# A two-layer transformer kernel on one core: reordered opening loads and norm, and a stage join without a meeting of all engines

## The reference

```python
h = rms_norm(x, attn_norm)
proj = einsum('bsd,dc->bsc', h, w_in)          # split into 17 parts
... fox attention, short convolution, mLSTM, windowed attention with a relative bias ...
x = x + merged @ w_merge_out
h = rms_norm(x, ffn_norm)
x = x + (silu(h @ w_gate) * (h @ w_up)) @ w_down       # ffn1
```

## Time and profile before

| | |
|---|---|
| median of 3 runs | 1770.75 us (1769.94 to 1770.77) |
| profiled execution | 1771.35 us, its span 1769.6 us |
| PE busy | 97% of the span |
| DVE, ACT, POOL busy | 54%, 48%, 54% |
| first matmul | 12.84 us |
| mean granted TensorE clock | 0.992 |

### The profile page before, as it was taken

One profiled execution on the slowest core, in us unless ns is written; L12 is line 12 of the kernel. 1 busy time (PEld: TensorE's weight loads), 2 busy tenths in 40 slices (PEclk: granted clock), 3 DMA queues, 4 the chain that ended last, 5 costly groups with the idle time before them and its releaser, 6 DMA issues. The chain is left out here.

```text
span 1769.6 us, 27618 instructions
## 1 busy us (share of the span) xinstructions
PE 1714.8 (97%) x10430; PEld 1523.5 (86%) x10430; DVE 956.7 (54%) x1628; ACT 845.3 (48%) x1686; POOL 963.8 (54%) x701
## 2 busy tenths in 40 slices
PE   6999999999999999999979999999999999999998
PEld 4898887888888998999868978888988889989996
DVE  2147554454538761575048469994324398528842
ACT  4234454332336551464236348884534566426642
POOL 2353432334444874677336449993752368648852
PEclk9999999999999999999989999999999999999999
DMA  6332221123351433233324321012442223323431
GB/s 223 96 84 54 64 74 51 51 61 101 107 176 55 120 111 104 84 96 126 113 65 136 108 64 57 2 37 71 141 125 69 72 84 96 126 78 96 120 120 48
DMA packets 222900, 162.09 MB, mean 92 GB/s; under 512 B 9768, under 2 KB 197296, under 8 KB 222768
## 3 DMA queue, kind: packets, MB, share of 16 engines
q1 hardware_dynamic: 221712, 159.26, 30.2%
q10 hardware_dynamic: 1056, 1.06, 0.2%
HBM read 156.09 MB, written 2.11 MB: 89 GB/s over the span
## 5 line engine op out<-in xcount | busy, mean ns | idle before, releaser
L352 POOL TENSOR_TENSOR w_low<-ring,w_high 128x1024 fp32r<-128x1024 f32 (+2 forms) x223 | 487.9, 2192 | 587.5 <-ACT w_high L344 587.1
L365 PE MATMUL psum<-hT,w_high 128*128 128x512 f32 (+1 forms) x1104 | 378.9, 343 | 7.3 <-PEq L184 6.1
L344 ACT ACTIVATE w_high<-ring 128x1024 fp32r<-128x1024 f32 (+2 forms) x223 | 212.1, 954 | 355.1 <-PE psum L367 354.9
L367 PE MATMUL psum<-hT,w_low 128*128 128x512 f32 (+1 forms) x1104 | 373.2, 338 | 0.0
L366 PE MATMUL psum<-hL,w_high 128*128 128x512 f32 (+1 forms) x1104 | 373.0, 338 | 0.0
L365 PEld LDWEIGHTS psum<-hT,w_high 128*128 128x128 f32 x1104 | 209.9, 190 | 28.7 <-issue 7.3
L367 PEld LDWEIGHTS psum<-hT,w_low 128*128 128x128 f32 x1104 | 209.5, 190 | 22.8
L366 PEld LDWEIGHTS psum<-hL,w_high 128*128 128x128 f32 x1104 | 210.0, 190 | 19.8
L1819 POOL TENSOR_TENSOR w_low<-ffn_sums,w_high 128x512 fp32r<-128x512 f32 x120 | 169.4, 1426 | 49.7 <-ACT w_high L1814 49.5
L365 PE MATMUL psum<-ffn_th,w_high 128*128 128x256 f32 x640 | 181.6, 284 | 4.7 <-DVE ffn_g L2067 3.1
L1819 POOL TENSOR_TENSOR w_low<-ring,w_high 128x512 fp32r<-128x512 f32 x120 | 155.7, 1300 | 54.7 <-ACT w_high L1814 48.8
(11 more groups left out here) (443 smaller groups left out, 3758.7 us busy)
## 6 DMA issues: line engine op xcount, KB each, us to landing
ring<-in_w_in SPq DMA_DIRECT2D x58, 512.0 KB, 3.6
ring<-in_ffn_w_up SPq DMA_DIRECT2D x44, 512.0 KB, 3.8
ring<-in_w_gate SPq DMA_DIRECT2D x22, 512.0 KB, 3.7
ring<-in_w_up SPq DMA_DIRECT2D x22, 512.0 KB, 4.8
ring<-in_w_down SPq DMA_DIRECT2D x20, 512.0 KB, 3.7
ring<-in_ffn_w_down SPq DMA_DIRECT2D x20, 512.0 KB, 3.8
ring<-in_nsa_w_in SPq DMA_DIRECT2D x18, 512.0 KB, 3.6
ring<-in_ca_wkv SPq DMA_DIRECT2D x16, 512.0 KB, 3.6
```

Source lines behind the costliest of these rows:

```text
L344: nc.scalar.activation(tile_view(w_high, n, SPLIT), tile_view(ring, n, RING), ACT.Copy).then_inc(w_hi, 1)
L352: nc.gpsimd.tensor_tensor(tile_view(w_low, n, SPLIT), tile_view(ring, n, RING), tile_view(w_high, n, SPLIT), ALU.subtract).then_inc(w_lo, 1)
L365: nc.tensor.matmul(ps, lhsT=sh, rhs=mh, start=first, stop=False)
L367: return nc.tensor.matmul(ps, lhsT=sl, rhs=mh, start=False, stop=last)
```

## The change

In the opening:

- SP loads x tile 0, the gain, the identity alone and weight tile 0 first, then x tiles 1 to 3, weight tiles 1 and 2, then the rest of the constants.
- ACT takes a square root of a constant at once, which loads its function table.
- Weight tile 0 is split in two halves. PE turns token tile 0, does the products of weight tile 0 for it (`first_tile`), turns token tile 1, and so on.
- The matmul of the bias rows moves from the start to the head of chunk 2; ACT's write and read of them and DVE's mirrored copy move behind it, the copy to chunk 3.

At the join:

- The block is not closed and no meeting is held. The semaphores of the mixers are cleared by POOL inside ffn1, those of ffn1 in the cross attention.
- ffn1d1 leaves token tile 3 to the sparse stage, and `early` lets ACT split one weight tile more before the last token tile's square.
- The sparse stage starts with the left halves (token tiles 0 and 1) of its first feature tile, turns token tile 3, does the left half of the second, and then both right halves.

```diff
+        def stage_ends():
+            done = list(stage_sems)
             stage_sems.clear()
+            return done
...
+            early = early or whole is not None
...
-                            if whole is not None and t == tiles - 2:
+                            if early and t == tiles - 2:
                                 split_high(a, n0 + per - min(SPLIT, per) + SPLIT + 2)
...
         @block.tensor
-            pe.wait_ge(loaded, 48)
-            pe.wait_ge(misc, 16)
-            pe.wait_ge(zeroed, 2)
-            nc.tensor.matmul(bank[7][0:SWA_H, 0:384], lhsT=relT[:, :], rhs=const[0:BUCKETS + 1, C_OH:C_OH + 384],
-                             start=True, stop=True).then_inc(bias_mm, 1)
+            def first_tile(t):
+
+                pe.wait_ge(anorm.low, 2 * t + 1)
+                for kk in range(2):
+                    if kk == 0:
+                        pe.wait_ge(first_low, 1)
+                    else:
+                        pe.wait_ge(w_lo, 1)
+                    mm = chunk_product(0, 0, kk, t, first_split)
+                return mm
+
+            pe.wait_ge(ident_in, 16)
             for t in range(NT):
                 anorm.turn(pe, t)
+                if t < NT - 1:
+                    first_tile(t)
+            first_tile(NT - 1).then_inc(w_used, 1)
...
+                if c == 2:
+                    pe.wait_ge(loaded, 48)
+                    pe.wait_ge(misc, 16)
+                    pe.wait_ge(zeroed, 2)
+                    nc.tensor.matmul(bank[7][0:SWA_H, 0:384], lhsT=relT[:, :], rhs=const[0:BUCKETS + 1, C_OH:C_OH + 384],
+                                     start=True, stop=True).then_inc(bias_mm, 1)
...
         @block.scalar
+            nc.scalar.activation(stat[:, 151:152], eps, ACT.Sqrt).then_inc(warmed, 1)
+
+            def split_first():
+
+                wait_loaded(a, 0)
+                to, src = tile_view(w_high, 0, SPLIT), tile_view(ring, 0, RING)
+                nc.scalar.activation(to[:, 0], src[:, 0], ACT.Copy).then_inc(first_high, 1)
+                nc.scalar.activation(to[:, 1], src[:, 1], ACT.Copy).then_inc(w_hi, 1)
+                state["high"] = 1
+
+            for t in range(NT):
+                a.wait_ge(x_in[t], 16)
+                anorm.square(a, t, 0, D)
+                anorm.root(a, t)
+                if t == 0:
+                    anorm.high_part(a, 0, (0,))
+                    split_first()
+                    anorm.high_part(a, 0, (1,))
+                if t >= 2:
+                    anorm.high_part(a, t - 1)
+            split_high(a, 2)
+            anorm.high_part(a, NT - 1)
             split_high(a, SPLIT)
...
             for c in range(n_chunks):
+                if c == 2:
+                    bias_rows_out()
                 split_high(a, chunk_tile[c + 1] + SPLIT - 1)
+                if c == 2:
+                    bias_rows_back()
...
         @block.vector
+            for t in range(NT):
+                anorm.scale(v, t)
+                if t != 1:
+                    anorm.low_part(v, max(t - 1, 0))
+            anorm.low_part(v, NT - 1)
...
                 if c == 3:
+                    v.wait_ge(bias_in, 32)
+                    nc.vector.tensor_copy(bias[:, :, :], bias_back[:, :, ::-1])
                     v.wait_ge(rooted, 1)
...
         @block.sync
+            load_tokens(0)
             anorm.load(sp)
+            sp.dma_start(ident, w['const'][:, C_ID:C_ID + P]).then_inc(ident_in, 16)
+            load_weights(sp, 1 - RING)
+            for t in range(1, NT):
+                load_tokens(t)
+            load_weights(sp, 3 - RING)
+            sp.dma_start(const[:, P:C_END], w['const'][:, P:C_END]).then_inc(loaded, 16)
...
+                    if sems_done:
+
+                        nc.clear_and_free_semaphores(sems_done)
                     for operand in ("A11", "S2", "S1", "A12"):
                         seven.low(g_, r1, operand)
...
-        middle.close()
-
-        clear_stage()
...
-            for i in range(4):
+            pe.wait_ge(norm_n.low, NT)
+            products(n0, 0, slice(0, HALF))
+            norm_n.turn(pe, NT - 1)
+            products(n0 + 1, 1, slice(0, HALF))
+            pe.wait_ge(norm_n.low, 2 * NT)
+            for i in range(2):
+                products(n0 + i, i, slice(HALF, S)).then_inc(w_used, 1)
+            for i in (2, 3):
                 feature(n0 + i, i)
```

More of the change, by code:

```diff
@@ L457, in _parts, with high_part @@
                         self.dst[0][:, four, cut], self.dst[1][:, four, cut])
-            def high_part(self, a, t):
-                for c in range(2):
+            def high_part(self, a, t, parts=range(2)):
+                for c in parts:
                     src, high, _ = self._parts(t, c)
@@ L1036, in _ @@
                     wait_chunk_out(pe, c - 2)
[L1037 to L1039 removed]
+                if c == 2:
[4 more added lines that the diff above has]
+                                     start=True, stop=True).then_inc(bias_mm, 1)
+                for s in range(1 if c == 0 else 0, width // P):
+                    tile = tile_for(pe, chunk_tile[c] + s, 'w_in')
                     for kk in range(1024 // width):
[L1041 removed]
                         for t in range(NT):
[L1043 to L1047 removed]
+                            if c == 0 and s == 2 and kk == 0:
                                 pe.wait_ge(anorm.low, 2 * t + 2)
[L1049 to L1051 removed]
+                            if c == 2 and s + kk == 0 and t == 3:
+                                pe.wait_ge(bias_row, 1)
+                            mm = chunk_product(c, s, kk, t, tile)
                     mm.then_inc(w_used, 1)
@@ L1240, in _ @@
             a.wait_ge(eps_set, 1)
-            for t in range(NT + 1):
-                if t < NT:
-                    a.wait_ge(x_in[t], 16)
-                    anorm.square(a, t, 0, D)
-                    anorm.root(a, t)
-                else:
-                    split_high(a, 1)
-                if t >= 1:
-                    anorm.high_part(a, t - 1)
-                if t == 1:
-                    a.wait_ge(bias_mm, 1)
-                    nc.scalar.activation(biasrow[:, :], bank[7][0:SWA_H, 0:384], ACT.Copy).then_inc(bias_row, 1)
-                    a.wait_ge(bias_row, 1)
-                    nc.scalar.dma_start(scratch_bias, biasrow[:, :]).then_inc(bias_out, 16)
@@ L1421, in _ @@
                 if c == 0:
-                    v.wait_ge(bias_in, 32)
-                    nc.vector.tensor_copy(bias[:, :, :], bias_back[:, :, ::-1])
+                    v.wait_ge(loaded, 48)
+                    nc.vector.tensor_copy(const_r[:, :], const_in[:, :])
                 if c == 1:
@@ L1649, in _ @@
             nc.gpsimd.memset(relT[BUCKETS:BUCKETS + 1, :], 1.0).then_inc(zeroed, 1)
+            g.wait_ge(zeroed, 2)
+            to, src, high_of = (tile_view(buf, 0, depth) for buf, depth in ((w_low, SPLIT), (ring, RING), (w_high, SPLIT)))
+            for kk in range(2):
+                if kk == 0:
+                    g.wait_ge(first_high, 1)
+                else:
+                    g.wait_ge(w_hi, 1)
+                nc.gpsimd.tensor_tensor(to[:, kk], src[:, kk], high_of[:, kk], ALU.subtract)\
+                    .then_inc(first_low if kk == 0 else w_lo, 1)
+            state["low"] = 1
             split_low(g, chunk_tile[4] + SPLIT)
@@ L2302, in _, with products, feature @@
         def _(pe):
-            def feature(n, b):
+            def products(n, b, cut):
                 wh, wl = tile_for(pe, n, 'nsa_w_in_2')
                 for k in range(ND):
-                    mm = product(bank[b][:, :], (wh[:, k, :], wl[:, k, :]), (hT[:, k, :], hL[:, k, :]), k == 0, k == ND - 1)
-                mm.then_inc(w_used, 1)
+                    mm = product(bank[b][:, cut], (wh[:, k, :], wl[:, k, :]), (hT[:, k, cut], hL[:, k, cut]), k == 0, k == ND - 1)
+                return mm
+            def feature(n, b):
+                products(n, b, slice(0, S)).then_inc(w_used, 1)
             def blocks(i):
@@ L2601, in _ @@
         def _(g):
+            g.wait_ge(norm_n.low, 1)
             nc.gpsimd.memset(kcp[:, :, :, P:P + 1], 0.0).then_inc(zeroed, 1)
```

69 lines of the change are left out of this document (30 added, 39 removed).

## The result

The changed kernel takes 1754.61 us (median of four runs, 1752.35 to 1755.42) against 1770.76 for the kernel before on the same chip: ratio 0.9913, interval 0.9901 to 0.9926, 16.2 us less. The forecast was 1758.3, 12.5 less. The profiled execution took 1752.35 us, the fastest of the four, its span 1750.5.

What follows compares the result with a forecast made beforehand. TensorE, busy 97% of the span, was taken as the bound. Opening 3.3 (4.3 less 0.8 and 0.2) plus join 9.2 made 12.5 us off 1771.35, 1758.9, or 1758.3 as median; 8-in-10 range 1751.5 to 1763.

Steps and rivals of the forecast that it cites:

- rival A: Opening: clock rises during it, near 19 to 22 us; second weight tile 4.5 us earlier than forecast, 1753.8; chance 0.20.
- Token tile 0: Opening: scaling starts at 6.3 us, transposes at 7.15, first three products at 10.95, all six done at 13.55.
- The clock in the opening: Opening: clock low until 30.8 to 32.9 us, second weight tile ends at 35.5 to 36.5; gain taken as 4.3 us.
- The bias product: Head of chunk 2: now on PE's path, 0.7 us plus 0 to 0.3 wait at token tile 3; loss 0.7 to 1.0.
- POOL beside DVE: Opening: POOL's halves of weight tile 0 run a fifth slower beside DVE's low parts; loss 0.2 us.
- The join without a fall: Join of ffn1 and sparse stage: two feature tiles done at 908.5 instead of 918.45, 10.0 us gained if the clock holds.
- With a fall: Join: clock falls in PE's 3.2 us pause, 1.6 us lost, gain 8.4; even chances, so 9.2 taken.
- The dips elsewhere (C): Later pauses: clock falls move as the program comes earlier, plus or minus 3 us, 1755.5 to 1761.5; counted inside forecast's 0.60.
- B: Join: left half waits or clock stays low over all four halves; gain only 1 to 4 us, 1764 to 1767; chance 0.12.
- D: Whole kernel: nothing changes, gain lost behind a transfer or bias wait, or pause due to profiling; 1767 to 1774; chance 0.05.
- E: Behind the join: 256-column products with a turn between keep the clock low into later feature tiles; slower, 1775; chance 0.03.

Runs made afterwards that it cites:

- e6: Changed kernel without ACT's early square root, so two table loads return to the opening's chain; 1756.02 us, ratio 0.9923 to the kernel before.
- e10: As e8, but POOL's first low part at the join waits until DVE has scaled token tile 2; 1755.79 us, ratio 0.9919 to the kernel before.
- e3: Changed kernel, but PE turns all four token tiles before the products of weight tile 0; 1756.44 us, ratio 0.9919 to the kernel before.
- e4: Changed kernel with no meeting, but token tile 3 turned in the down stage and features whole, as before; 1757.40 us, ratio 0.9927 to the kernel before.
- e8: Changed kernel; ACT splits the first feature tile before token tile 2's square, token tile 3 turned mid second left half; 1757.42 us, ratio 0.9933 to kernel before.
- e9: As e8, with the bias product also moved into PE's pause before token tile 2's products in the opening; 1756.18 us, ratio 0.9924 to the kernel before.
- e2: Changed kernel with the opening taken back, so the join change alone; 1761.58 us, ratio 0.9956 to the kernel before.

## Why the prediction was right, and where it was off

The time lies in the range, 3.7 us under the forecast, and the join was forecast by the right mechanism. The opening was not: what happened there is rival A, to which the prediction gave 0.20, and the time is in the range because the range took A in. In the profiled pair the span falls by 19.1 us, 6.6 more than the 12.5 of the forecast. That the medians miss by only 3.7 is luck in part: it rests on executions slower than the profiled one.

- **Token tile 0.** Transposes at 7.22 (7.15 forecast), first product 11.02 (10.95), next transposes 13.71 (13.55). The start of the scaling, 6.32 for 6.3, was right because two errors met: x tile 0 had landed at 4.11 and not at 4.56, and DVE then waited 0.5 us for the gain, a wait that the prediction doesn't have. The removed table loads were worth what was said: e6 puts them back, 2.64 us on the first transposes.
- **The clock in the opening: the step that failed.** "So I take it as low until 26.8 plus 4.0 to 6.1". The first weight tile was to end at 29.4 and ended at 24.37. In none of the twelve profiled executions with the new opening or a variant of it did the clock rise as late as 30.8. In the eight with the change's order of turns and products, the early square root and no added products it rose between 14 and 20.5 us, in e6, where the chain starts 2.64 later, at 24.02 at the latest. The term was 4.3 and measured 10.45; over those eight it ranges from 8.1 (e10, second weight tile at 32.39) to 10.45. This is rival A, and it went further than A's 8.8. The error was in the reading: two rises were timed from the first product after a pause, and the transposes right before were taken as worth nothing. e3 shows a rise 1.85 us after the first product when no pause lies between, and e4, e8, e9 and e10 show it inside a run of transposes. The rule that was cited for the forecast (the Trainium skill, TensorE: Matmul & The Clock Gate, HAM oscillation) is about bursts of matmuls that are shorter than the waits between them; there each burst starts low. The prediction carried it over to bursts of 2.6 us parted by waits of 0.75, and for such the traces show the other: with pauses of 0.97 us between them the bursts stayed at 2.4 GHz from 15.90 on.
- **The bias product.** 0.74 us on the path (0.7 to 1.0, taken 0.8), with no wait at its fourth token tile, and no late weight tile behind ACT's wait for the row.
- **POOL beside DVE.** Taken as 0.2 lost; nothing was. Two halves took POOL 2.50 us at 9.61, 1.25 each, against 1.29 for one in the earlier trace rows, with DVE's low parts beside them. The 2.83 us of the earlier trace rows had been read as low parts slowing POOL; it is the scaling that does it. In the change POOL's first subtraction at the join, which starts during the scaling of 881.18, takes 2.84 of the 5.20; in e10, where it starts behind the scaling and has DVE's low parts beside it, 2.36. The rule of the Trainium skill (GPSIMD Engine Reference, Specifications) that contention comes from VectorE instructions with two SBUF inputs had given nearly 0, and the trace agrees with it: the scaling has x and the gain in SBUF, the low part has one operand in PSUM.
- **The join without a fall: 10.0 forecast, 9.96 measured** in the profiled execution. The left half started 0.15 after POOL's subtraction (0.05 forecast), the transposes of tile 3 ran at once behind it, and neither clear of semaphores showed in the waits of PE. **With a fall: 8.4 forecast**; e2 gives 25.72 less 17.12, 8.6. Even chances were taken; over the executions it fell in five of seven, in neither of the two of the change itself.
- **The dips elsewhere (C)** moved as allowed for, plus 1.3 and minus 1.85 in the profiled pair.

The sum with measured terms is 10.45 less 0.74, plus 9.96, plus 1.3, less 1.85: 19.1, which is the difference of the spans. The medians differ by less, 16.2; the profiled execution is the fastest of its four. In the variants the clock rises later in the opening or falls at the join (the table's two last columns: 2.3 and 1.4 us). That the other executions of the change lose their time in these ways isn't shown, since only profiled executions have a trace.

Rivals B, D and E did not occur: no wait took the place of the meeting, and nothing stayed at the low clock past the first left half.

What stays open: what decides, with the same work in the same order, whether the clock rises at 14 or at 20 us, or falls at the join in spite of equal waits; and why the falls near 1040 and 1425 move and change their length when the work ahead ends some microseconds earlier. No run was made for the latter. In the opening, the order of the loads was not changed alone.

## What to carry to other kernels

Look for work that is ready while the bound engine waits for a chain of others, and cut it so that it fits into the pause: here the left halves in the pause were worth 6.0 us, more than the meeting of all engines that stood beside it (3.95). When a pause costs the clock, price both levels, and ask of each trace what ran right before the rise, transposes included. Before an elementwise operation of one of DVE and POOL is moved ahead, see what the other does at that time: the early split of e8 looked free, and the join took 4.7 us longer.

## What the runs showed of the hardware

- DVE's scaling of 512 columns, with both operands in SBUF, takes 0.75 us alone. When it starts during a subtraction of POOL, it ends about 0.55 us behind the end of that: 4.65 us for two in e8, 2.87 in e10, 2.68 in the change. DVE's low part of the same size, with one operand in PSUM, keeps its 0.68 beside the same subtractions. When the scaling starts first, POOL is the one that takes longer, 2.84 instead of 2.40.
- With the same order of work, the granted clock rose at different times (weight tile 0 done from 24.37 to 26.66 in eight profiled executions of the change and its variants, with 1.86 us of waiting before the first product in each). The two of the change itself agree to 0.04 us, so that one program's own executions differ in this isn't shown.
- The clock can rise during transposes: in e4, e8, e9 and e10 it did so inside a run of eight.
- In the change, DVE's first reciprocal was released by the transfer of the gain, 0.5 us after ACT's root: the 0.5 MB gain, not x, ended the chain's last wait for a transfer.
- Float32 products of zeros, issued from 1.29 us on, had TensorE at 2.4 GHz for its first transposes at 7.27.
